# Reordered chunk work in the mLSTM heads, and its transfers issued by SyncE

## The chip, the core and the metric

The kernel runs as one program on one core of a Trainium2 chip. The metric is the device time of that program in microseconds (us). Five engines take part: TensorE (PE in the rows; PEld is its weight load), VectorE (DVE), ScalarE (ACT), GpSimd (POOL) and SyncE (SP), which here only issues transfers. Each has its own queue of instructions, worked off in order; they meet at semaphores.

## The reference, cut to what matters

Two layers of a decoder run over 1024 prompt tokens with 16 meta tokens ahead of them, and over 8 sample sequences of 4 tokens. The second layer is an mLSTM with 4 heads of width 512. The prompt goes in chunks of 128 tokens, one after another, because each chunk reads the matrix state C (512 x 512) that the chunk ahead left:

```python
num = w_inter[..., None] * jnp.einsum('bhtd,bhde->bhte', q, C) + jnp.einsum('bhts,bhse->bhte', s, v)
C_new = decay[..., None, None] * C + jnp.einsum('bhsd,bhse->bhde', k * w_s[..., None], v)
n_new = decay[..., None] * n + jnp.einsum('bhs,bhsd->bhd', w_s, k)
```

The first term of `num` is the **inter** part (through the old state), the second the **intra** part (within the chunk). Each of the 8 sample sequences has its own C of 1 MB a head, which is read, multiplied, updated and written back.

## The kernel before, in words

The stages run one after another: the attention layer, its output, the input projections of the mLSTM layer (`pre`), the four **heads** (function `heads`, from L1509), and the output stage (`post`). The change touches `heads` alone. For a head `e` it does this:

- **Values.** Nine tiles of 128 tokens (the first, of 48, holds sample and meta tokens): TensorE multiplies in three passes (high times high, high times low, low times high, helper `three`, L1690 to L1692) into banks 6 and 7 in turn; ScalarE copies the high part out (`high_v`, L1869), VectorE the low part (`low_v`, L1987). ScalarE and VectorE split the input x in the same way ahead of that (`high_x`, `low_x`), and the input c, which the projections need, at the last four tiles (`high_c`, `low_c`, tiles 5 to 8).
- **Projections.** Four blocks of keys and four of queries (`project`).
- **Chunks 0 to 7.** A chunk c has on TensorE: `scores`, `turn_keys` (transposes), `sample_parts` (reads the state `Cs` of sample c), then `inter` (four multiplications with C, with the four `sample_state` multiplications between them), `intra`, and `prompt_state` (four units of three passes). The results of `sample_state` and `prompt_state` are called units; they go alternately to banks 2 and 3, so that TensorE may write unit u only when VectorE has taken unit u-2 (`kv_done`). VectorE takes them in the order of its own code: `sample_states`, `numerator`, `prompt_states`. `numerator` is three instructions: inter part times a column (L2126), plus the intra part (L2127), and `bn_stats` on the sum (L2129).
- Chunk 0 has no inter part. Its `prompt_state` also adds the 48 first tokens (twelve more passes), and `small` makes some sums of one column and the sample sequences' own scores.
- After chunks 4 and 6 VectorE also splits the next head's weights (`low_w`, L1995).

**Transfers.** SyncE issues the loads of a head: c, the gate rows (`ub`, `nrow`, `ws`), `w_q`, and the next head's x, `w_k`, `w_v`. GpSimd issues all that belongs to the states: the loads of the sample states into the two halves of `Cs`, their stores, the stores of the numerators (`num`), and at a head's end C, n and the sample numerators. The load of c for head e+1 (L1621) waits for TensorE's last unit of head e; the gate rows wait for the stores of n.

Of the kernel before, what the change touches and what calls it, by code (L numbers as in the profile page):

```python
# [13 lines left out]
P = 128  # L14
# [1111 lines left out]
def seq(i):  # L1126

    return slice(SQ + P * i, SQ + P * (i + 1))
# [380 lines left out]
def heads(nc, d, const, cols, metaw, decay8, gate_dram, x_dram, ca_dram, num_dram, mv, den):  # L1509
# [5 lines left out]
    with ExitStack() as ctx:  # L1515
# [45 lines left out]
        kv_full, kv_done, small_full, small_done, num_full, num_done = (  # L1561
            s.sem(n) for n in ("kv_full", "kv_done", "small_full", "small_done", "num_full", "num_done"))
# [22 lines left out]
        def _(sp):  # L1585
# [44 lines left out]

            load_v(0)
            load_x(0)
            load_k(0)
            for e in range(HC):
                load_c(e)
                load_rows(e)
                load_w(e)
                load_q(e)
                if e + 1 < HC:
                    load_x(e + 1)  # L1640
                    load_k(e + 1)
                    load_v(e + 1)

        @block.gpsimd
        def _(pool):
            old = d["state_C"].rearrange("l b h (k p) c -> (l b) h p k c", p=P)
            new = d["out_C_s"].rearrange("l b h (k p) c -> (l b) h p k c", p=P)
            pool.memset(qm[:, :, :, :], 0.0).then_inc(qm_zero, 1)
            for e in range(HC):
                cc = slice(DH * e, DH * (e + 1))  # L1650

                def load(b):
                    pool.dma_start(Cs[:, b % 2], old[b, e]).then_inc(cs_in[b % 2], 16)

                def store_num(c):
                    pool.wait_ge(num_done, NT * e + c + 1)
                    pool.dma_start(num_dram[c, :, cc], num[:, c % 2, :]).then_inc(num_out[c % 2], 16)

                pool.wait_ge(p_full, NJ * (e + 1))
                for b in range(2):  # L1660
                    load(b)
                for b in range(B):
                    pool.wait_ge(kv_done, NU * e + s_unit(b, KH - 1) + 1)
                    pool.dma_start(new[b, e], Cs[:, b % 2]).then_inc(cs_out[b % 2], 16)
                    if b >= 1:
                        store_num(b - 1)
                    if b + 2 < B:
                        pool.wait_ge(cs_out[b % 2], 16 * (B // 2) * e + 16 * (b // 2) + 16)
                        load(b + 2)
                store_num(NT - 1)  # L1670
                pool.wait_ge(kv_done, NU * (e + 1))
                pool.dma_start(d["out_C_p"].rearrange("l b h (k p) c -> (l b h) p k c", p=P)[e], C[:, :, :]).then_inc(c_out, 16)
                with nc.allow_non_contiguous_dma(reason="512 words"):
                    for m in range(KH):
                        pool.dma_start(d["out_n_p"].rearrange("l b h (k p o) -> (l b h) p k o", p=P, o=1)[e, :, m],
                                       nall[:, m, NT - 1:NT]).then_inc(n_out, 16)
                pool.dma_start(d["out_n_s"].rearrange("l b h c -> (l b) (h c)")[:, cc], nrow[:, :]).then_inc(n_out, 16)
                pool.wait_ge(fold_done, e + 1)
                pool.dma_start(num_dram[NT, 0:NS, cc], s_num[:, :]).then_inc(snum_out, 16)
            for j in range(2):  # L1680
                pool.wait_ge(num_out[j], 16 * (NT // 2) * HC)
                pool.wait_ge(cs_out[j], 16 * (B // 2) * HC)
            pool.wait_ge(c_out, 16 * HC)
            pool.wait_ge(n_out, 16 * (KH + 1) * HC)
# [800 lines left out]
```

## Time and profile before

| | us |
|---|---|
| median of 3 runs | 2527.56 (2524.15 to 2535.24) |
| the profiled execution, whole | 2520.63 |
| its span in the trace | 2518.9 |
| TensorE busy in the span | 2147.9 (85%) |
| VectorE / ScalarE / GpSimd busy | 1096.5 / 632.9 / 94.4 |
| the heads, from the first value tile | 1446 to 2256 |

### The profile page before, as it was taken

How to read it: one execution, taken by the hardware profiler on the slowest of the kernel's cores; microseconds unless marked ns; L12 is line 12 of the kernel's file. 1: busy time of each engine (PE TensorE's matmuls, PEld its weight loads, DVE VectorE, ACT ScalarE, POOL GpSimd, SP SyncE). 2: the span in 40 equal slices, each digit the busy share in tenths (PEclk: the TensorE clock that was granted, in tenths of full speed). 3: DMA queues.
4: the chain of work that ended last, by engine and by line, in shares of the span. 5: the costliest groups of instructions: out<-in, count | busy, mean ns of one | idle time of the engine just before them, and what ended most of it. 6: DMA issues, size and time to landing. Idle time of an engine off the chain costs nothing. (4 is left out here: it accounts for less than half of the span.)

```text
span 2518.9 us, 28050 instructions
## 1 busy us (share of the span) xinstructions
PE 2147.9 (85%) x10945; PEld 1567.4 (62%) x10945; DVE 1096.5 (44%) x1868; ACT 632.9 (25%) x1088; POOL 94.4 (4%) x149
## 2 busy tenths in 40 slices
PE   4989888879956599899999598889889989965998
PEld 3655555544433244899999586576567558544885
DVE  4151515241222122353443345845764675566442
ACT  3151524240021111332222232121132122015221
POOL 0000000000000000000000000100110110110000
PEclk8999999989987799899999898998998899897999
DMA  3101010033066321586575413542542351448561
GB/s 114 28 24 39 11 51 0 18 95 113 0 183 207 122 67 39 91 114 155 128 132 148 192 71 108 185 148 101 177 180 91 130 184 37 144 156 296 180 184 34
DMA packets 180240, 281.80 MB, mean 112 GB/s; under 512 B 15283, under 2 KB 114615, under 8 KB 179018
## 3 DMA queue, kind: packets, MB, share of 16 engines
q1 hardware_dynamic: 151013, 183.12, 26.8%
q0 software_dynamic: 24256, 88.82, 9.8%
q10 hardware_dynamic: 4864, 8.39, 1.1%
q8 instruction: 72, 1.18, 0.2%
q14 instruction: 35, 0.29, 0.0%
HBM read 185.17 MB, written 95.31 MB: 111 GB/s over the span
## 5 line engine op out<-in xcount | busy, mean ns | idle before, releaser
L1263 PE MATMUL pre_ps<-x_xh,pre_wh 128*128 128x358 f32 (+1 forms) x792 | 260.0, 328 | 13.1 <-DVE pre_wl L1385 13.1
L1264 PE MATMUL pre_ps<-norm_xl,pre_wh 128*128 128x358 f32 (+1 forms) x792 | 258.5, 326 | 0.0
L1265 PE MATMUL pre_ps<-x_xh,pre_wl 128*128 128x358 f32 (+1 forms) x792 | 258.3, 326 | 0.0
L389 PE MATMUL attn_ps<-x_xnT,attn_w 128*128 128x512 f32 (+1 forms) x576 | 193.9, 498 | 9.9 <-DMA attn_w<-in_w_in_a 8.0
L389 PEld LDWEIGHTS attn_ps<-x_xnT,attn_w 128*128 128x128 f32 x576 | 97.1, 194 | 106.6 <-issue 98.4
L1263 PEld LDWEIGHTS pre_ps<-x_xh,pre_wh 128*128 128x128 f32 x792 | 149.5, 189 | 14.6 <-DVE pre_wl L1385 13.7
L1264 PEld LDWEIGHTS pre_ps<-norm_xl,pre_wh 128*128 128x128 f32 x792 | 149.5, 189 | 0.0
L1265 PEld LDWEIGHTS pre_ps<-x_xh,pre_wl 128*128 128x128 f32 x792 | 149.4, 189 | 0.0
L649 PE MATMUL pool_ps<-x_xnT,pool_w 128*128 128x512 f32 (+1 forms) x384 | 131.2, 505 | 13.8 <-DMA pool_w<-in_w_in_a 8.8
L1028 PE MATMUL norm_yp<-norm_wo,even_mixT 128*128 128x512 f32 (+1 forms) x288 | 127.8, 603 | 15.5 <-DMA norm_wo<-in_w_out_a 15.5
L1690 PE MATMUL head_ps<-head_ch,head_wh 128*128 128x358 f32 (+1 forms) x384 | 128.1, 334 | 12.2 <-issue 9.1
L2287 PE MATMUL post_ps<-post_woh,post_oh 128*128 128x512 f32 (+1 forms) x288 | 114.9, 399 | 17.1 <-DVE post_ol L2381 16.3
L1691 PE MATMUL head_ps<-head_cl,head_wh 128*128 128x358 f32 (+1 forms) x384 | 127.6, 332 | 0.0
L1692 PE MATMUL head_ps<-head_ch,head_wl 128*128 128x358 f32 (+1 forms) x384 | 127.2, 331 | 0.0
L2099 DVE SCALAR_TENSOR_TENSOR head_Cs<-head_Cs,head_ub,head_ps 128x512 f32<-128x512 f32 x128 | 93.9, 747 | 56.9 <-PE head_ps L1784 56.9
L1825 PE MATMUL head_ps<-head_C,head_q 128*128 128x512 f32 x224 | 117.2, 605 | 0.0
L649 PEld LDWEIGHTS pool_ps<-x_xnT,pool_w 128*128 128x128 f32 x384 | 65.5, 197 | 79.3 <-issue 70.4
L2288 PE MATMUL post_ps<-post_wol,post_oh 128*128 128x512 f32 (+1 forms) x288 | 113.3, 393 | 0.0
L2289 PE MATMUL post_ps<-post_woh,post_ol 128*128 128x512 f32 (+1 forms) x288 | 113.3, 393 | 0.0
L573 DVE TENSOR_TENSOR_SCAN attn_rest<-attn_neg 128x1040 f32<-128x1040 f32 (+8 forms) x72 | 89.9, 1249 | 47.1 <-ACT attn_neg L505 46.5
L1028 PEld LDWEIGHTS norm_yp<-norm_wo,even_mixT 128*128 128x128 f32 (+1 forms) x288 | 53.5, 188 | 84.2 <-issue 68.5
L1926 ACT ACTIVATE head_sTh<-head_sT 128x128 fp32r<-128x128 f32 x32 | 9.8, 308 | 364.6 <-DVE head_sT L2077 364.6
(374 smaller groups left out, 3803.7 us busy)
## 6 DMA issues: line engine op xcount, KB each, us to landing
head_Cs<-in_state_C POOLq DMA_DIRECT2D x32, 1024.0 KB, 5.8
out_C_s<-head_Cs POOLq DMA_DIRECT2D x32, 1024.0 KB, 4.7
x_xnT<-in_cache_sb_k SPq DMA_DIRECT2D x64, 256.0 KB, 2.9
pre_w<-in_w_in_c SPq DMA_DIRECT2D x32, 512.0 KB, 9.7
x_dram<-low_low SPq DMA_DIRECT2D x16, 536.0 KB, 9.7
ca_dram<-low_low SPq DMA_DIRECT2D x16, 536.0 KB, 10.6
b_dram<-pre_bv SPq DMA_DIRECT2D x16, 536.0 KB, 7.6
a_dram<-low_low SPq DMA_DIRECT2D x16, 536.0 KB, 7.6
```

Source lines behind the costliest of these rows:

```text
L389: last = pe.matmul(ps[:, bank + c, 0:c1 - c0], w[:, u, k, :], xnT[:, k, c0:c1], start=(k == 0), stop=(k == KD - 1))
L649: last = pe.matmul(ps[:, bank + c, 0:c1 - c0], w[:, g % 2, a, k, :], xnT[:, k, c0:c1], start=(k == 0), stop=(k == KD - 1))
L1028: last = pe.matmul(yp[0:rows, q, half, :], tok(mixT[:, k, :], i), wo[:, k, BANK * half:BANK * (half + 1)], start=(k == 0), stop=(k == KD - 1))
L1263: pe.matmul(out, wh[:, t % 2, k, :], xh[:, k, c0:c1], start=(k == 0), stop=False)
L1264: pe.matmul(out, wh[:, t % 2, k, :], xl[:, k, c0:c1], start=False, stop=False)
L1265: last = pe.matmul(out, wl[:, t % 2, k, :], xh[:, k, c0:c1], start=False, stop=(k == KD - 1))
L1690: pe.matmul(out, ah, bh, start=start, stop=False)
L1691: pe.matmul(out, ah, bl, start=False, stop=False)
L1692: return pe.matmul(out, al, bh, start=False, stop=stop)
L1825: pe.matmul(ps[:, 4, :], q[:, k, seq(c)], C[:, k, :], start=(k == 0), stop=(k == KH - 1))
L2287: pe.matmul(out, high, woh[:, k, c], start=(k == 0), stop=False)
L2288: pe.matmul(out, high, wol[:, k, c], start=False, stop=False)
```

## The change

1. **Chunk 0.** `prompt_state`, `small` and `intra` now come before `sample_parts` and `sample_state` on TensorE, and VectorE takes them in that order (`s_unit` and `c_unit` number the units anew to suit).
2. **Numerator.** ScalarE now does the multiplication of the inter part (`decayed`, a new function, between `high_keys(c)` and `own_keys(c+1)`); VectorE only adds. `bn_stats` (`moments`) comes after `prompt_states`.
3. **Split of c.** One tile earlier: tiles 4 to 7, and ahead of the copy of the tile's values instead of behind it.
4. **Head's end.** `low_x(e+1, 0)` and `low_x(e+1, 1)` come before the numerator of chunk 7. Value tile 0 uses bank 7, tile 1 bank 6, so that the wait for the denominators moves from tile 0 to tile 1.
5. **Transfers.** SyncE issues all that GpSimd did, in one queue with its loads. The state loads and stores of head e come after `load_v(e+1)`; the load of c for head e+1 comes after C's and n's stores of head e.

```diff
         def s_unit(b, m):
-            return 2 * KH * b + m
+            return 2 * KH * b + m + KH * (b == 0)
         def c_unit(c, m):
-            return 2 * KH * c + KH + m
+            return 2 * KH * c + m + KH * (c >= 1)
...
+            def states(e):
+                sp.wait_ge(p_full, NJ * (e + 1))
+                for b in range(2):
+                    load_state(e, b)
+                for b in range(B):
+                    sp.wait_ge(kv_done, NU * e + s_unit(b, KH - 1) + 1)
+                    sp.dma_start(new[b, e], Cs[:, b % 2]).then_inc(cs_out[b % 2], 16)
+                    if b >= 1:
+                        store_num(e, b - 1)
+                    if b + 2 < B:
+                        sp.wait_ge(cs_out[b % 2], 16 * (B // 2) * e + 16 * (b // 2) + 16)
+                        load_state(e, b + 2)
+                store_num(e, NT - 1)
+                sp.wait_ge(kv_done, NU * (e + 1))
+                sp.dma_start(d["out_C_p"].rearrange("l b h (k p) c -> (l b h) p k c", p=P)[e], C[:, :, :]).then_inc(c_out, 16)
...
                 load_w(e)
+                if e >= 1:
+                    store_sample(e - 1)
                 load_q(e)
                 if e + 1 < HC:
                     load_x(e + 1)
                     load_k(e + 1)
                     load_v(e + 1)
+                states(e)
...
                 if n == 0:
                     pe.wait_ge(wlv, e + 1)
                     if e >= 1:
-                        pe.wait_ge(den_done, e)
                         pe.wait_ge(parts_done, e)
+                elif n == 1 and e >= 1:
+                    pe.wait_ge(den_done, e)
...
+            def decayed(e, c):
+                act.wait_ge(i_full, (NT - 1) * e + c)
+                if c >= 2:
+                    act.wait_ge(num_out[c % 2], 16 * (NT // 2) * e + 16 * (c // 2))
+                    act.wait_ge(bn_done, NT * e + c - 1)
+                act.activation(num[:, c % 2, :], ps[:, 4, :], ACT.Copy, scale=hcol(Q_INTER, c, e)).then_inc(i_done, 1)
...
                 for n in range(NV):
                     if n + 2 < NV:
                         high_x(e, n + 2)
+                    if n >= KH and n < 2 * KH:
+                        high_c(e, n - KH)
                     high_v(e, n)
-                    if n >= NV - KH:
-                        high_c(e, n - NV + KH)
...
                 low_scores(e, 0)
                 log_weights(e, 1)
+                prompt_states(e, 0)
+                sample_small(e)
+                numerator(e, 0)
                 sample_states(e, 0)
-                sample_small(e)
-                prompt_states(e, 0)
-                numerator(e, 0)
+                moments(e, 0)
...
                     sample_states(e, c)
+                    if c == NT - 1 and e + 1 < HC:
+                        low_x(e + 1, 0)
+                        low_x(e + 1, 1)
                     numerator(e, c)
                     prompt_states(e, c)
+                    moments(e, c)
```

VectorE, one chunk from 1 on, before (`Cs` is a sample state, `C` the prompt's, `kwl` the keys' low part):

```order
L2091 SCALAR_TENSOR_TENSOR head_kwl<-head_ps,all_cols,head_kwh 128x512
L2099 SCALAR_TENSOR_TENSOR head_Cs<-head_Cs,head_ub,head_ps 128x512 x4
L2126 TENSOR_SCALAR head_num<-head_ps,all_cols 128x512
L2127 TENSOR_TENSOR head_num<-head_num,head_ps 128x512
L2129 BN_STATS head_bn<-head_num 128x6
L2109 SCALAR_TENSOR_TENSOR head_C<-head_C,head_ub,head_ps 128x512 x4
```

And now:

```order
L2112 SCALAR_TENSOR_TENSOR head_kwl<-head_ps,all_cols,head_kwh 128x512
L2120 SCALAR_TENSOR_TENSOR head_Cs<-head_Cs,head_ub,head_ps 128x512 x4
L2146 TENSOR_TENSOR head_num<-head_num,head_ps 128x512
L2130 SCALAR_TENSOR_TENSOR head_C<-head_C,head_ub,head_ps 128x512 x4
L2150 BN_STATS head_bn<-head_num 128x6
```

Of the three instructions between the sample's units and the prompt's, one is left there.

TensorE behind the scores of chunk 0, before (`qm` are the samples' queries, `kb` their keys, `ks` and `qn` belong to `small`):

```order
L1762 MATMUL head_ps<-head_q,head_kz 128x128 x4
L1772 MATMUL head_ps<-head_Cs,head_qm 32x512 x4
L1784 MATMUL head_ps<-head_vs,head_kb 128x512 x4
L1799 MATMUL head_ps<-head_ks,all_const 8x512
L1802 MATMUL head_ps<-all_const,head_qn 128x1 x7
```

And now, behind the same scores (the first five rows), then from the end of `small` to the end of the chunk:

```order
L1769 MATMUL head_ps<-head_q,head_kz 128x128 x4
L1696 MATMUL head_ps<-head_vh,head_kwh 128x512
L1697 MATMUL head_ps<-head_vl,head_kwh 128x512
L1698 MATMUL head_ps<-head_vh,head_kwl 128x512
L1696 MATMUL head_ps<-head_vh,head_kmh 128x512
```

```order
L1698 MATMUL head_ps<-head_vh,head_sTl 32x512
L1696 MATMUL head_ps<-head_vh,head_sTh 128x512
L1697 MATMUL head_ps<-head_vl,head_sTh 128x512
L1698 MATMUL head_ps<-head_vh,head_sTl 128x512
L1826 MATMUL head_ps<-all_const,head_sT 128x1
L1696 MATMUL head_ps<-head_vh,head_sTh 128x512
L1697 MATMUL head_ps<-head_vl,head_sTh 128x512
L1698 MATMUL head_ps<-head_vh,head_sTl 128x512
L1828 MATMUL head_ps<-all_const,head_sT 128x1
L1779 MATMUL head_ps<-head_Cs,head_qm 32x512 x4
L1790 MATMUL head_ps<-head_vs,head_kb 128x512 x4
```

The reading of `Cs` has moved from the first place to the last, and `intra` (the rows with `sTh`, 128x512) now follows `small` at once.

SyncE at the end of head 0, before:

```order
L1597 DMA head_w<-in_w_v 128x4x512
L1621 DMA head_cr<-ca_dram 128x4x1072
L1612 DMA head_ub<-gate_dram 128x1088
L1613 DMA head_nrow<-in_state_n 8x512
L1629 DMA head_ws<-gate_dram 128x1072
```

And now:

```order
L1647 DMA out_C_s<-head_Cs 128x4x512
L1639 DMA num_dram<-head_num 128x512 x2
L1655 DMA out_C_p<-head_C 128x4x512
L1658 DMA out_n_p<-head_nall 128x1 x4
L1660 DMA out_n_s<-head_nrow 8x512
L1621 DMA head_cr<-ca_dram 128x4x1072
L1612 DMA head_ub<-gate_dram 128x1088
```

The load of c (`cr`) now stands behind six issues that were another engine's.

## Rows read from the trace of the kernel before

**Rows 1.** Busy time of one stretch, the heads: PE, PEld, DVE, ACT, POOL, clock, DMA share, GB/s.

```profile
1446.00:2256.00 810.00, 726.07 (x3408) 530.72 (x3408) 500.47 (x829) 176.86 (x320) 80.86 (x123) 0.93 0.38 134
```

**Rows 2.** TensorE's waits in the heads (total us, times, longest), then one group by line.

```profile
PE head_ps L1690 <- DVE head_C L2109: 40.8, 28, 1.5
PE head_ps L1690 <- DVE head_xl L1981: 32.7, 4, 27.2
PE head_ps L1772 <- DMA head_Cs<-in_state_C: 16.6, 4, 4.8
...
L1690 PE MATMUL head_ps<-head_ch,head_wh 128*128 128x358 f32 (+1 forms) x384 | 128.1, 334 | 12.2 <-issue 9.1 <-DVE head_cl L1991 3.1
```

**Rows 3.** Timeline of VectorE, chunk 4 of head 0: start, length, instruction, [idle before].

```profile
1603.01 0.75 DVE L2126 TENSOR_SCALAR head_num<-head_ps,all_cols 128x512 f32<-128x512 f32 x1
...
1604.51 0.69 DVE L2129 BATCH_NORM_STATS2 head_bn<-head_num 128x6 f32<-128x512 f32 x1
1605.12 1.39 DVE L2109 SCALAR_TENSOR_TENSOR head_C<-head_C,head_ub,head_ps 128x512 f32<-128x512 f32 x2
```

**Rows 4.** Timeline of TensorE, from chunk 3's like release to chunk 4's.

```profile
1593.64 0.50 PE L1690 MATMUL head_ps<-head_vh,head_kwh 128*128 128x512 f32 x1 [1.47 <-DVE head_C L2109]
...
1600.91 1.02 PE L1825 MATMUL head_ps<-head_C,head_q 128*128 128x512 f32 x2
...
1604.06 0.39 PE L1692 MATMUL head_ps<-head_vh,head_kwl 128*128 128x512 f32 x1
1605.91 0.50 PE L1690 MATMUL head_ps<-head_vh,head_kwh 128*128 128x512 f32 x1 [1.47 <-DVE head_C L2109]
```

**Rows 5.** Chunk 0 of heads 0 to 3, scores to scores: us, PE busy, clock, DMA.

```profile
1525.92:1556.44 30.52, 25.18 (x100) 0.73 0.49 172
1727.21:1759.06 31.85, 27.09 (x99) 0.66 0.44 165
1930.51:1965.51 35.00, 29.84 (x99) 0.57 0.42 150
2136.50:2163.70 27.20, 23.69 (x100) 0.76 0.44 155
```

**Rows 6.** The same view of a stretch within head 3's chunk 0.

```profile
2151.00:2167.00 16.00, 16.00 (x45) 0.50 0.20 66
```

**Rows 7.** Timelines of TensorE and VectorE around `small`, head 0.

```profile
1538.75 1.72 PE L1802 MATMUL head_ps<-all_const,head_qn 128*128 128x1 f32 x14
1541.80 0.73 DVE L2115 SCALAR_TENSOR_TENSOR head_nrow<-head_nrow,all_decay,head_ps 8x512 f32<-8x512 f32 x1 [3.15 <-PE head_ps L1692]
1542.47 0.67 DVE L2116 COPY head_s_num<-head_ps 32x512 f32<-32x512 f32 x1
```

**Rows 8.** The first projections of heads 1 and 3: us, PE busy, clock, DMA.

```profile
1676.00:1713.00 37.00, 36.71 (x215) 0.95 0.30 108
2085.00:2122.00 37.00, 36.43 (x214) 0.95 0.06 24
```

**Rows 9.** Timeline of VectorE after chunk 4 of head 0.

```profile
1608.25 2.28 DVE L1995 TENSOR_TENSOR head_wl<-head_w,head_wh 128x2048 fp32r<-128x2048 f32 x1
```

**Rows 10.** The page's DMA issues (KB each, us to landing), then timelines of SP and ACT.

```profile
head_Cs<-in_state_C POOLq DMA_DIRECT2D x32, 1024.0 KB, 5.8
out_C_s<-head_Cs POOLq DMA_DIRECT2D x32, 1024.0 KB, 4.7
head_cr<-ca_dram SPq DMA_DIRECT2D x4, 2144.0 KB, 16.6
...
1645.55 0.37 SPq L1621 DMA_DIRECT2D head_cr<-ca_dram  x1
...
1665.46 1.09 ACT L1876 ACTIVATE head_ch<-head_cr 128x1072 fp32r<-128x1072 f32 x1
```

**Rows 11.** Timelines of POOL and SP around the end of the heads.

```profile
2256.22 0.53 POOL L1679 DMA_DIRECT2D num_dram<-head_s_num  x1
2269.45 0.32 SPq L2235 DMA_DIRECT2D post_num<-num_dram  x1
```

More of the change, by code:

```diff
@@ L1629, in load_w, with load_state, store_num, store_sample @@
                 sp.dma_start(ws[:, :], gate_dram[e:e + 1, XT + NT + B:GW].to_broadcast([P, XT])).then_inc(ws_in, 16)
+            old = d["state_C"].rearrange("l b h (k p) c -> (l b) h p k c", p=P)
+            new = d["out_C_s"].rearrange("l b h (k p) c -> (l b) h p k c", p=P)
+            def load_state(e, b):
+                sp.dma_start(Cs[:, b % 2], old[b, e]).then_inc(cs_in[b % 2], 16)
+            def store_num(e, c):
+                sp.wait_ge(num_done, NT * e + c + 1)
+                sp.dma_start(num_dram[c, :, DH * e:DH * (e + 1)], num[:, c % 2, :]).then_inc(num_out[c % 2], 16)
+            def states(e):
[13 more added lines that the diff above has]
+                sp.dma_start(d["out_C_p"].rearrange("l b h (k p) c -> (l b h) p k c", p=P)[e], C[:, :, :]).then_inc(c_out, 16)
+                with nc.allow_non_contiguous_dma(reason="512 words"):
+                    for m in range(KH):
+                        sp.dma_start(d["out_n_p"].rearrange("l b h (k p o) -> (l b h) p k o", p=P, o=1)[e, :, m],
+                                     nall[:, m, NT - 1:NT]).then_inc(n_out, 16)
+                sp.dma_start(d["out_n_s"].rearrange("l b h c -> (l b) (h c)")[:, DH * e:DH * (e + 1)], nrow[:, :]).then_inc(n_out, 16)
+            def store_sample(e):
+                sp.wait_ge(fold_done, e + 1)
+                sp.dma_start(num_dram[NT, 0:NS, DH * e:DH * (e + 1)], s_num[:, :]).then_inc(snum_out, 16)
             load_v(0)
@@ L1642, in _ @@
                     load_v(e + 1)
+                states(e)
+            store_sample(HC - 1)
+            for j in range(2):
+                sp.wait_ge(num_out[j], 16 * (NT // 2) * HC)
+                sp.wait_ge(cs_out[j], 16 * (B // 2) * HC)
+            sp.wait_ge(c_out, 16 * HC)
+            sp.wait_ge(n_out, 16 * (KH + 1) * HC)
+            sp.wait_ge(snum_out, 16 * HC)
         @block.gpsimd
         def _(pool):
-            old = d["state_C"].rearrange("l b h (k p) c -> (l b) h p k c", p=P)
@@ L1647, in _ @@
-            new = d["out_C_s"].rearrange("l b h (k p) c -> (l b) h p k c", p=P)
             pool.memset(qm[:, :, :, :], 0.0).then_inc(qm_zero, 1)
[L1649 to L1684, printed above, removed]
-            pool.wait_ge(snum_out, 16 * HC)
         @block.tensor
@@ L1705, in value_tile @@
                 for k in range(KH):
-                    last = three(ps[0:rows, 6 + n % 2, :], xh[:, k, c], xl[:, k, c], wh[:, 0, k, :], wl[:, 0, k, :], k == 0, k == KH - 1)
+                    last = three(ps[0:rows, 7 - n % 2, :], xh[:, k, c], xl[:, k, c], wh[:, 0, k, :], wl[:, 0, k, :], k == 0, k == KH - 1)
                 last.then_inc(v_full, 1)
@@ L1822, in inter @@
                 pe.wait_ge(num_done, NT * e + c)
+                if c >= 2:
+                    pe.wait_ge(i_done, (NT - 1) * e + c - 1)
                 for k in range(KH):
                     pe.wait_ge(kv_done, NU * e + c_unit(c - 1, k) + 1)
-                    pe.matmul(ps[:, 4, :], q[:, k, seq(c)], C[:, k, :], start=(k == 0), stop=(k == KH - 1))
+                    last = pe.matmul(ps[:, 4, :], q[:, k, seq(c)], C[:, k, :], start=(k == 0), stop=(k == KH - 1))
+                    if k == KH - 1:
+                        last.then_inc(i_full, 1)
                     sample_state(e, c, k)
@@ L1838, in _ @@
                 scores(e, 0)
+                prompt_state(e, 0)
+                small(e)
+                intra(e, 0)
                 sample_parts(e, 0)
@@ L1841, in _ @@
                     sample_state(e, 0, m)
-                small(e)
-                prompt_state(e, 0)
-                intra(e, 0)
                 for c in range(1, NT):
@@ L1868, in high_v @@
                 act.wait_ge(v_full, NV * e + n + 1)
-                act.activation(vh[0:rows, i, :], ps[0:rows, 6 + n % 2, :], ACT.Copy).then_inc(vh_done, 1)
+                act.activation(vh[0:rows, i, :], ps[0:rows, 7 - n % 2, :], ACT.Copy).then_inc(vh_done, 1)
             def high_c(e, k):
@@ L1965, in _ @@
                     high_keys(e, c)
+                    decayed(e, c)
                     if e + 1 < HC:
@@ L2152, in _ @@
             for e in range(HC):
-                low_x(e, 0)
-                low_x(e, 1)
+                if e == 0:
+                    low_x(e, 0)
+                    low_x(e, 1)
                 for n in range(NV):
@@ L2157, in _ @@
                         low_x(e, n + 2)
+                    if n >= KH and n < 2 * KH:
+                        low_c(e, n - KH)
                     low_v(e, n)
```

24 lines of the change are left out of this document (12 added, 12 removed).

## The prediction

> **What bounds the kernel now.** I read the page first: TensorE is busy for 85% of the span. Then the stretch of the heads, the only one that the change touches [rows 1]: 810 us, of which TensorE is busy for 726, VectorE for 500, ScalarE for 177. So TensorE sets this stage, and it can become shorter in two ways: its idle time (84 us) goes, or its clock, 0.93 on the mean, rises. Third, the waits of TensorE say whose fault the idle time is [rows 2]: 40.8 us in 28 waits are for VectorE's update of C, 32.7 for the low part of x (27.2 of them once, before head 0, which the change leaves alone, so 5.5 in three), 16.6 in four for the first sample state, and 12.2 before the first projection. Each of the four has its own edit. All the edits lie inside the 810 us.
>
> **The numerator (edit 2).** In a chunk VectorE does L2126, L2127, L2129 and only then the first update of C [rows 3]. TensorE has meanwhile finished two units of the prompt's state, at 1604.06 + 0.39 = 1604.45, and may start the third only at 1605.91, when the first has been taken [rows 4]: 1.47 us of idle, in each of the 28 chunks from 1 to 7. Now only the addition stands there. It could start at 1603.01, where L2126 does, if ScalarE's product is ready. The last inter multiplication ends at 1600.91 + 1.02 = 1601.93 and ScalarE has nothing else to do; the nearest row for its copy of 512 columns is the 0.75 of L2126, so the product is there at about 1602.8. The update of C then starts one spacing later (1604.51 to 1605.12 is 0.61), at 1603.65, and TensorE may go on 0.79 later (1605.12 to 1605.91), at 1604.44. That is when its second unit ends, so the whole 1.47 goes and the period, from 1593.64 to 1605.91 [rows 4] or 12.27 us, becomes 10.8, TensorE's own work. VectorE, busy for 500 of 810 us and rid of 28 times 0.75, can follow. In 25 chunks this is 25 x 1.46 = **36.4**. Not in the last chunk of heads 0 to 2: there the two `low_x` stand ahead of the addition, and they wait for ScalarE's product, its copy of the parts and its high parts of x. VectorE gets to the addition some 1.9 us later than it would, so the stall is about 1.9 us, 0.5 more than now: 3 x 0.5 = **-1.5**. And the cover of `low_w` becomes thin: it lasts 2.28 us [rows 9], `bn_stats` (0.69) now also stands ahead of it, and the chunk is shorter by 1.46. I work out a stall of 1.3 us at the third sample unit where now there is 0.3: six chunks, **-6.0**. `bn_stats` itself costs nothing elsewhere: VectorE waits there for the next scores.
>
> **The end of a head (edit 4).** With the low parts of x ready and the denominators no longer asked for, value tile 0 follows the last prompt unit at once: **+5.5** [rows 2]. Tile 1 gets its denominators: they take 0.7 us behind VectorE's last update, and tile 0 takes 2.9.
>
> **The split of c (edit 3).** Its last low part now comes before the last tile's values, so the first projection starts at once: **+12.2** [rows 2]. In heads 1 to 3 the clock is below 1.00 just behind that wait, 0.95 in 37 us in two of them [rows 8] and a little lower in the third, about 2 us of lost work each: **+6.0**.
>
> **Chunk 0 (edit 1).** Its four stretches add up to 124.6 us [rows 5]. In head 0, 30.52 us at a mean clock of 0.73 are 16.5 us at half clock, so the 25.18 us busy are 17 us of work at full clock; head 3 gives 17 as well. To these 17 the new order adds a wait for the keys' low part (new: the scores end and nothing stands between; about one VectorE instruction of 0.75 and two releases, 1.1), one of 1.5 (new: `intra` needs VectorE's 0.73 + 0.67 [rows 7], which `prompt_state` covered before), and some 1.4 for the samples' units, which go at VectorE's pace: 21.0 us, or 84 for four. The wait for `Cs` is gone, since the state has 13 us more to arrive in. So the gain is 41 us if the clock stays up. It did not stay up: it is 0.57 to 0.76 in these stretches, and in head 3, where TensorE was busy all the time, it stood at 0.50 for 16 us on end [rows 6]. What lay ahead of that fall was the thin work of `small`, 14 matmuls of one column in 1.72 us [rows 7], after a wait of 2.8 us. The new order still has `small`, with a wait right behind it, and then the narrow sample work. I expect a fall there too, later and partly over waits: 10 to 13 us at half clock, some 5 us lost a head. That gives 41 - 21 = **+20**. The ends are +41 (no fall) and +7 (a full fall of 17 us on dense work in each head, 4 x 8.5 lost).
>
> The Trainium skill, page "TensorE: Matmul & The Clock Gate", section "Why this matters for your kernels", says that idle gaps between bursts, such as a wait for a DMA, put the engine back to its lower rate. Head 3's row speaks against this as the whole story: the clock was low while nothing waited. By the rule alone, chunk 0 would give the 41 us.
>
> **The transfers (edit 5).** Most of it is hidden. A state's store and the next load on the same half of `Cs` take 4.7 + 5.8 = 10.5 us [rows 10]; from the sample's update to the next need for that half there are about 15 us in the shorter chunks, and 12 for the first. SyncE has nothing else queued in the chunks. The place to look at is the load of c for the next head. Before it was issued at 1645.55, 0.5 us behind TensorE's last unit, and landed 16.6 us later in the median [rows 10], at about 1662; ScalarE took it at 1665.46 and did not wait. Now six issues stand ahead of it on SyncE (C, four of n, one more), about 0.4 us each, and C's megabyte ahead of it in the queue; and ScalarE comes to it sooner: now 18.6 us behind the start of the value tiles, then a tile of 2.8 us earlier and some 2.0 us more because it goes ahead of the tile's copy, so 13.8 us behind the start, which is the end of the last unit; TensorE feels a delay from 1.5 us on. The bytes in flight are the same as before. If small stores of n no longer hold it up it lands at 13 to 14 us and costs nothing; if it keeps its longest landing of 17.5 us on top of an issue 3.3 us late, TensorE waits 6 us a head. I take 0.7 a head, nearer to the lower end since bandwidth is left over (DMA share 0.38 [rows 1]): **-2**, ends 0 and -18. Last, GpSimd's final store was issued at 2256.22 and the next stage started at 2269.45 [rows 11]; SyncE issues faster than the 0.53 us of GpSimd: **+2**, ends 0 and +5.
>
> "DMA: Bandwidth & Descriptors" in the Trainium skill, section "Issuing engines are not separate DMA queues", says that who issues changes only the time of the issue. That fits a small term here, and no run so far shows it.
>
> **Sum.** 36.4 - 1.5 - 6.0 + 5.5 + 12.2 + 6.0 + 20 - 2 + 2 = 72.6 us. The profiled execution took 2520.6, so it would take 2448. The median of the runs lies 7 us above the profiled one; I expect the same of the new kernel: **2455 us**.
>
> **The rivals.**
> *The clock stays up in chunk 0.* For it: three of the four waits for `Cs` were over 4 us and go. Against it: head 3. It gives 21 us more: 2434.
> *The clock falls as long as before, and c comes late.* For it: `small` is now followed by more narrow work; c's load is behind a queue. Chunk 0 gives 7 instead of 20 and c costs 18 instead of 2: 29 us less, 2484.
> *The stall changes its place.* The addition waits for ScalarE's product (it has a release from TensorE, 0.7 us of work and a release to VectorE in it), and edit 2 brings nothing: the 36.4 go, 2491. Against it: 1.1 us lie between the end of inter and 1603.01.
> *Slower than before: state loads come late in the single queue.* Each of the 24 reloads has a chain of store, numerator store, wait and load in one queue. It costs nothing up to 15 us and then each us costs TensorE one. All gains are spent when each reload is late by 72.6 / 24 = 3 us, a chain of 18 us where the rows give 10.5. Against it: the DMA share of 0.38.
>
> **How the numbers follow.** My forecast 60%, the clock up 15%, clock and c 10%, the stall in a new place 8%, slower 4%, and 3% for something smaller near no change. The range takes in the first three and the edge of the fourth: 2430 to 2490. A measurement of this kernel tells some 0.5% (12.6 us) from no change. Faster by more than that: 93%; within it 3%; slower 4%.
>
> **What would show it.** Of the profile of the changed kernel: the waits for the update of C should be about 3 instead of 28, near 1.9 us each; a chunk's period 10.8 us; no wait for `Cs` before chunk 0's parts, but one of 1.1 and one of 1.5 us in each; no idle time before the first projection and its clock at 1.00; chunk 0 from scores to scores near 26 us. A wait of ScalarE for the load of c, with TensorE idle at value tile 6, would show the c term larger. The prediction is wrong if the clock in chunk 0 is up all the time (too high) or if a transfer shows among TensorE's longest waits (too low).

## The result, and the profile after

The changed kernel takes **2460.06 us** (median of 4 runs, 2455.93 to 2475.11) where the kernel before took 2525.99 (4 runs, 2524.15 to 2535.24). The ratio is 0.9743, with a 95% interval of 0.9695 to 0.9791. The forecast was 2455 with a range of 2430 to 2490. The profiled execution took 2455.93 us, its span 2454.2, so 64.7 us less than the span before.

First the heads, in the view of [rows 1], then their chunks 0 in that of [rows 5]: us, PE, PEld, DVE, ACT, POOL busy, clock, DMA share, GB/s.

```profile
1446.00:2192.00 746.00, 700.49 (x3407) 514.26 (x3405) 473.33 (x784) 195.07 (x348) 0.00 (x0) 0.95 0.42 143
1521.56:1546.44 24.88, 21.79 (x99) 12.72 (x100) 11.40 (x25) 2.69 (x7) 0.00 (x0) 0.79 0.35 126
1709.73:1734.83 25.10, 21.92 (x99) 12.96 (x100) 11.39 (x25) 2.69 (x7) 0.00 (x0) 0.80 0.34 125
1900.14:1925.19 25.05, 22.11 (x100) 12.93 (x101) 11.43 (x25) 2.69 (x7) 0.00 (x0) 0.78 0.36 125
2089.54:2113.76 24.22, 21.00 (x100) 12.56 (x100) 11.40 (x25) 2.69 (x7) 0.00 (x0) 0.86 0.24 87
```

TensorE's idle time fell from 84 to 46 us, and its clock rose from 0.93 to 0.95. What it still waits for, as in [rows 2] (total us, times, longest), and then, from the groups by line, the first pass of the projections:

```profile
PE head_ps L1696 <- DVE head_vl L2008: 17.6, 3, 6.6
PE head_ps L1696 <- DVE head_C L2130: 7.4, 21, 1.5
PE head_ps L1790 <- DVE head_Cs L2120: 6.2, 13, 0.6
PE head_ps L1696 <- DVE head_s_num L2137: 6.1, 4, 1.5
PE head_ps L1696 <- DVE head_kwl L2112: 4.0, 4, 1.0
```

```profile
L1696 PE MATMUL head_ps<-head_ch,head_wh 128*128 128x358 f32 (+1 forms) x384 | 125.1, 326 | 0.0
```

The waits for C went from 40.8 to 7.4 us, those for the sample state and before the projections are gone. At the top stands one that was not there: VectorE's low part of the values, three times, 5.2 to 6.6 us each. It is the load of c. This is the boundary from head 0 to head 1 on SyncE, ScalarE, VectorE and TensorE, in order of time:

```profile
1627.48 0.39 SPq L1655 DMA_DIRECT2D out_C_p<-head_C  x1
1627.91 3.31 SPq L1658 DMA_DIRECT2D out_n_p<-head_nall  x4
1631.26 0.34 SPq L1660 DMA_DIRECT2D out_n_s<-head_nrow  x1
1631.76 0.39 SPq L1621 DMA_DIRECT2D head_cr<-ca_dram  x1
1640.62 0.33 SPq L1612 DMA_DIRECT2D head_ub<-gate_dram  x1
...
1646.66 1.10 ACT L1889 ACTIVATE head_ch<-head_cr 128x1072 fp32r<-128x1072 f32 x1 [6.53 <-DMA head_cr<-ca_dram]
...
1649.72 0.79 PE L1696 MATMUL head_ps<-head_wh,head_xh 128*128 128x512 f32 x1 [5.19 <-DVE head_vl L2008]
```

ScalarE stands at the split of c from 1640.1 on, and the next copy of a value tile is queued behind it; VectorE's low part follows that copy, and TensorE follows VectorE. The DMA windows of the same boundary say what the load was doing:

```profile
1628.00:1631.00 3.00, 3.00 (x15) 2.11 (x14) 2.10 (x9) 1.11 (x2) 0.00 (x0) 1.00 0.88 330
1631.00:1640.00 9.00, 9.00 (x38) 6.38 (x37) 5.44 (x17) 3.22 (x6) 0.00 (x0) 1.00 0.85 46
1641.00:1649.00 8.00, 3.53 (x16) 2.54 (x14) 1.21 (x2) 2.34 (x4) 0.00 (x0) 0.92 0.92 370
```

The store of C moves at 330 GB/s; then for 9 us the DMA engines count as busy at a share of 0.85 and move 46 GB/s; then c comes at 370. In the 9 us stand some 600 packets of four bytes, the 512 words of n among them, which themselves take 5 us of engine time out of 122; nearly all the rest are 75 packets of c, at 1.5 us each where they take 0.17 later on. So the load of c has begun and hardly moves while n, issued ahead of it on the same queue, is being stored. The gate rows (`ub`) wait for n's stores, and are issued at 1640.62: that is when these are over.

**Where the 64.7 us are.** From one `scores` to the next, the periods of the two traces give: chunks 0 124.6 to 99.3 us (25.3); chunks 1 56.4 to 45.1 (11.2); chunks 2 to 6 246.5 to 222.6 (23.9); chunk 7 of head 3 1.3; the three boundaries, from chunk 7 to the next head's first scores, 286.0 to 291.2 (**-5.2**); the start of head 0 3.4; from TensorE's end to the next stage's first load 16.7 to 13.8 (2.9); other stages 1.9.

### The profile page after: what moved, and what is told of

Same layout as the page of the kernel before. It is cut to its first block and busy times, and to the rows that moved or that the text cites. A ratio compares the mean times of both kernels' runs of the same rounds, so it can differ in the third digit from the quotient of the medians.

```text
span 2454.2 us, 28078 instructions
## 1 busy us (share of the span) xinstructions
PE 2120.6 (86%) x10945; PEld 1549.6 (63%) x10945; DVE 1073.3 (44%) x1840; ACT 651.4 (27%) x1116; POOL 12.8 (1%) x25
## 5 line engine op out<-in xcount | busy, mean ns | idle before, releaser
L1263 PEld LDWEIGHTS pre_ps<-x_xh,pre_wh 128*128 128x128 f32 x792 | 149.6, 189 | 14.6 <-DVE pre_wl L1385 13.7
L1697 PE MATMUL head_ps<-head_cl,head_wh 128*128 128x358 f32 (+1 forms) x384 | 125.1, 326 | 0.0
L1696 PE MATMUL head_ps<-head_ch,head_wh 128*128 128x358 f32 (+1 forms) x384 | 125.1, 326 | 0.0
L1698 PE MATMUL head_ps<-head_ch,head_wl 128*128 128x358 f32 (+1 forms) x384 | 124.9, 325 | 0.0
L1790 PE MATMUL head_ps<-head_vs,head_kb 128*128 128x512 f32 x128 | 96.5, 761 | 6.2 <-DVE head_Cs L2120 6.2
## 6 DMA issues: line engine op xcount, KB each, us to landing
x_dram<-low_low SPq DMA_DIRECT2D x16, 536.0 KB, 10.1
```

Source lines behind the costliest of these rows:

```text
L1263: pe.matmul(out, wh[:, t % 2, k, :], xh[:, k, c0:c1], start=(k == 0), stop=False)
L1696: pe.matmul(out, ah, bh, start=start, stop=False)
L1697: pe.matmul(out, ah, bl, start=False, stop=False)
L1698: return pe.matmul(out, al, bh, start=False, stop=stop)
```

## The experiments

All times are medians of 4 runs (e4 of 10), each beside runs of the kernel before (2522 to 2524); edits are against the changed kernel where nothing else is said.

**e1_c_first and e2_n_behind_c** move the load of c, **e3_pool_issues** and **e4_only_sync** take the transfers' part alone. In e1 c goes ahead of C's store, in e2 between C and n (head 0's c is then loaded ahead of the loop over the heads):

```diff
                 store_num(e, NT - 1)
+                if e + 1 < HC:
+                    load_c(e + 1)
                 sp.wait_ge(kv_done, NU * (e + 1))
```

```diff
                 sp.dma_start(d["out_C_p"].rearrange("l b h (k p) c -> (l b h) p k c", p=P)[e], C[:, :, :]).then_inc(c_out, 16)
+                if e + 1 < HC:
+                    load_c(e + 1)
                 with nc.allow_non_contiguous_dma(reason="512 words"):
```

> The changed kernel, but SyncE issues the load of c for the next head ahead of the stores of C and n of the head that ends (right behind the last numerator's store). Theory A (the 17.6 us that TensorE waits at value tile 6 in three heads come from the place of the load of c in the single queue): the load is issued within 1 us of TensorE's last unit, lands some 8 us later, ScalarE no longer waits for it, the three waits of 5.2, 6.6 and 5.9 us go, and with them the half-clock stretch of 6.8 us behind each: 20 to 26 us less than the changed kernel, about 2436. Theory B (the two splits that now stand ahead of the value copies hold TensorE up by themselves): the waits stay above 3 us each and the time stays within 8 us of 2460.

> The changed kernel, but the load of c for the next head stands between the store of C and the five stores of n, so that C's megabyte is still ahead of it and the 512 writes of 4 bytes are behind. Theory A1 (it is the small writes of n that hold the queue: while they run it moves 60 GB/s for about 9 us): c lands 3 us later than with c in front, some 11 us behind TensorE's last unit, before ScalarE asks for it at 13.8, and all the time of the other run is won, 2436 to 2440. Theory A2 (bytes and issue time of what stands ahead): C's store takes 2.8 of the 6 us, so about half of the wait stays, 2 to 4 us a head, and the time is 2446 to 2450.

e1: 2443.29 us, ratio 0.9679 (0.9643 to 0.9714). e2: 2438.65, 0.9676 (0.9643 to 0.9709). By the medians 16.8 and 21.4 us came back; the changed kernel's interval (0.9695 to 0.9791) is wide and just touches both, but the traces agree: the three boundaries take 274.5 and 271.1 us where they took 291.2. Part of it is clock: the three waits of the changed kernel are each followed by 6.8 to 10.2 us at half clock, and e2 has one such stretch left, of 3.4 us. e1 fell short of what was expected of it (20 to 26 us, no wait left): waits of 4.0 and 1.2 us for the value tile remain, in e2 one of 3.2. ScalarE at the first boundary, in e1, then in e2:

```profile
1647.26 1.10 ACT L1891 ACTIVATE head_ch<-head_cr 128x1072 fp32r<-128x1072 f32 x1 [5.36 <-DMA out_C_p<-head_C]
```

```profile
1644.93 1.10 ACT L1891 ACTIVATE head_ch<-head_cr 128x1072 fp32r<-128x1072 f32 x1 [4.55 <-DMA head_cr<-ca_dram]
```

In e1 c was in after 9 us, but its high part goes where C lies, and C's store now came last, 17.9 us after its issue and with n's stores right behind it. The two transfers must both be over, and at this boundary neither order frees the split; at the third boundary both do.

In e3 GpSimd issues the state transfers again, as before the change; e4 is the kernel before with only these functions moved to SyncE, so its diff is the same with the signs turned:

```diff
-                states(e)
-            store_sample(HC - 1)
...
         def _(pool):
...
+                for b in range(2):
+                    load(b)
+                for b in range(B):
+                    pool.wait_ge(kv_done, NU * e + s_unit(b, KH - 1) + 1)
+                    pool.dma_start(new[b, e], Cs[:, b % 2]).then_inc(cs_out[b % 2], 16)
...
```

> The changed kernel with edit 5 undone: GpSimd issues the states, numerators and final states as before, and SyncE only the loads; edits 1 to 4 stay. If the load of c lands as it did before (14 to 17.5 us behind its issue, 0.5 us behind TensorE's last unit) while it is asked for at 13.8, TensorE waits 1 to 4 us in each of three heads instead of 6: 7 to 12 us less than the changed kernel, 2448 to 2453, that is, edit 5 costs time on balance. Rival: the transfers by GpSimd delay sample states in the shorter chunks, so that waits for Cs come back and the time is over 2465.

> The kernel before with edit 5 alone: SyncE issues all, nothing else is changed. The load of c is asked for 20.4 us behind TensorE's last unit there and would land at about 20, so TensorE waits 0 to 1 us a head; the end of the heads stage is 3 us shorter; the wait for the first sample state keeps its 4 us: 2519 to 2528, no change that can be told. If the late load of c or the waits for Cs grow, it is slower than before by up to 15 us.

e3: 2450.38 us, 0.9721 (0.9689 to 0.9752), with two waits for the value tile of 6.1 us together instead of three of 17.6. e4: 2518.34, 0.9985 (0.9968 to 1.0003), with the waits of [rows 2] nearly as they were. **So the move to one queue costs nothing in the kernel before and, by the medians, 9.7 us in the changed one.** The intervals of e3 and the changed kernel overlap, so the size is not certain; the direction is borne out by the traces, in which the three boundaries take 275.5 us in e3 and 291.2 in the changed kernel (286.0 before, 285.7 in e4). The shorter boundary needs c earlier, and the move brings it later: 5.1 us behind TensorE's last unit instead of some 0.5.

**e5_numerator_undone, e6_chunk0_undone, e7_split_late** each take one edit back: in e5 VectorE multiplies the inter part again, with `bn_stats` right behind the sum; in e6 chunk 0 stands in its old order on TensorE and VectorE; in e7 c is split at value tiles 5 to 8 again.

```diff
-            act.activation(num[:, c % 2, :], ps[:, 4, :], ACT.Copy, scale=hcol(Q_INTER, c, e)).then_inc(i_done, 1)
...
+                    link(dve.tensor_scalar(dst, ps[:, 4, :], hcol(Q_INTER, c, e), None, ALU.mult))
```

```diff
-                prompt_state(e, 0)
-                small(e)
-                intra(e, 0)
                 sample_parts(e, 0)
                 for m in range(KH):
                     sample_state(e, 0, m)
+                small(e)
+                prompt_state(e, 0)
+                intra(e, 0)
```

```diff
-                    if n >= KH and n < 2 * KH:
-                        high_c(e, n - KH)
                     high_v(e, n)
+                    if n >= NV - KH:
+                        high_c(e, n - NV + KH)
```

> The changed kernel with edit 2 undone: VectorE multiplies, adds and takes bn_stats ahead of the prompt's units, ScalarE's decayed is gone; the rest stays. Theory (a third of a chunk's update stood in TensorE's way): the waits for the update of C come back in all 28 chunks, the period goes from 10.98 to 12.27 us, and the time rises by 25 x 1.29 = 32 us to 38 us, to about 2495. Rival (VectorE's order was not what set the period; the other edits would have brought it): the time rises by less than 15 us.

> The changed kernel with edit 1 undone: chunk 0 reads and updates the sample state first, then small, the prompt's units and intra. Theory (the wait for the first state, 4 times 3 to 5 us, and the 17 us at half clock that lie on the dense units): the four chunks 0 take 120 to 126 us again instead of 99, chunk 1 begins at half clock, and the time rises by 25 to 32 us to about 2488. Rival (the clock falls anyway, only elsewhere, so that only the wait itself counts): the rise is 10 to 15 us, about 2473.

> The changed kernel with edit 3 undone: the high and low parts of c are made at value tiles 5 to 8, behind the tile's copies; the load of c keeps its late place. Theory: c is asked for some 4.8 us later and TensorE feels a delay later still, so the waits at the value tiles shrink from 17.6 us to under 4, while the wait before the first projection comes back, 3 us in each of four heads: the two cancel, 2452 to 2462. Rival (the split's earlier place is worth its 12 us whatever c does): over 2468.

e5: 2488.7 us, 0.9860 (0.9837 to 0.9883); the period is 12.27 us again and 28 waits for C add up to 43.1. The numerator is worth 28.6 us, a little under the 32 to 38 expected. e6: 2494.27, 0.9881 (0.9860 to 0.9902); the four waits for the sample state are back (16.4 us), and chunk 0 takes 35.2, 35.0, 35.1 and 27.1 us. The order of chunk 0 is worth 34.2, over the 25 to 32 expected. e7: 2454.62, 0.9724 (0.9699 to 0.9749). Of its waits, the one ahead of the projections in heads 1 to 3:

```profile
PE head_ps L1696 <- issue: 9.1, 3, 3.0
```

The late split brings back 12.2 us ahead of the projections (these 9.1 and 3.1 in one head) and their lower clock (332 ns a matmul for 326). It cuts the waits for the value tile from 17.6 to 2.0 us, with no half clock behind them (23.9 us in the changed kernel, 3.4 in each of these heads now behind the projections' wait), and its median is 5.4 us *lower* than that of the changed kernel. The intervals overlap, so that it is faster is not shown; but no run shows a gain from edit 3 as the change has it. That it pays with c early is likely, since e2 has no wait ahead of the projections and only one of 3.2 us at a value tile, but no run has the late split with c early.

**e8 to e10: what brings the clock down in chunk 0.** In the changed kernel it is at half for 6.8 to 13.7 us in each chunk 0, from behind `small` (14 matmuls of one column) and a wait of 1.5 us for `s_num`. e8 is e2 with `small` between the second and the third prompt unit, so that VectorE has time for `s_num`; e9 is e8 with the one-column sums taken out of `small`, one to each later chunk; e10 is e2 with only this. The first diff is that of e8 and e9, the second that of e9 and e10:

```diff
-                prompt_state(e, 0)
+                prompt_state(e, 0, (0, 1))
                 small(e)
+                prompt_state(e, 0, (2, 3))
```

```diff
-                for c in range(1, NT):
-                    pe.matmul(ps[:, 6, 80 + c:81 + c], qn[:, P * (c - 1):P * c], one, start=True, stop=True)
...
                     intra(e, c)
+                    one_column(e, c)
                     prompt_state(e, c)
```

> The kernel with the load of c ahead of n's stores, and besides small stands between the second and the third of chunk 0's prompt units, on TensorE and on VectorE. Theory: the wait of 1.5 us at intra goes in each head (VectorE copies small's results under two units), 6 us in all, and the clock's fall, if thin work followed by a wait brings it about, comes later or is shorter: 6 to 15 us less than the kernel without this, 2424 to 2433. Rival (the thin work alone brings the fall about): the half-clock stretches in chunk 0 keep their 7 to 14 us and now lie on the two dense units, so only 0 to 3 us are won, or up to 5 lost.

> This is e8_small_between with the one-column sums of the function small taken out of it and spread: each later chunk's sum stands behind that chunk's second prompt unit, and the four for the sample rows in chunk 1. Theory (TensorE's fall to half clock is brought on by thin work, the one-column sums above all, also where the engine has no gap): in e8 the clock was at half for 13.7, 13.7, 27.3 and 13.7 us from right behind small, and chunk 0 took 25.7, 25.65, 29.6 and 25.7 us. With the sums gone from there most of the fall goes: at most 7 us at half in each head, chunk 0 at 18.5 to 21 us (at full clock its work is what 99 to 107 us in four heads less about half of 10 to 27 us each leaves), and the time 15 to 28 us under e8's 2442, 2414 to 2427. Rival 1 (the other thin work of the chunk, products with 8, 32 and 48 rows or columns, brings the fall by itself): chunk 0 stays at 24 to 27 us and the time within 5 us of e8's. Rival 2 (the sums bring it wherever they stand): falls turn up in the later chunks, the period there rises above 10.98 us, and the time is at or over e8's.

> This is e2_n_behind_c with the same one-column sums spread over the later chunks, and with small where the changed kernel has it. Here the waits for VectorE's kwl (1.0 us) and s_num (1.5 us) stand in chunk 0, as in the changed kernel, but the sums don't. If the sums bring the fall: the stretches at half clock in chunk 0 (10.2, 3.4 or 6.8, 10.2, 13.7 us) go, chunk 0 falls from some 25 to 20 us in each head, and the time is 10 to 20 us under e2's 2438.7, 2419 to 2429. If the waits bring it: chunk 0 is as in e2 and the time within 4 us of 2438.7, while e9, which has no such wait, is faster. If either is enough together with the thin products of 8 to 48 columns: both e9 and e10 stay where they were.

e8: 2442.21 us, 0.9672 (0.9639 to 0.9704). The wait for `s_num` is gone and nothing was won, as its rival had it. TensorE's timeline in head 0, then windows of TensorE alone (us, PE busy, clock, DMA):

```profile
1528.81 1.72 PE L1813 MATMUL head_ps<-all_const,head_qn 128*128 128x1 f32 x14
1530.46 0.41 PE L1815 MATMUL head_ps<-all_const,head_qs 128*32 128x1 f32 x8
1530.80 0.25 PE L1817 MATMUL head_ps<-all_const,head_sT 32*32 32x1 f32 x2
1530.98 0.63 PE L1698 MATMUL head_ps<-head_vh,head_sTh 32*32 32x512 f32 x1
```

```profile
1528.81:1542.00 13.19, 13.19 (x50) 0.58 0.07 28
```

TensorE has no idle moment from 1528.81 to 1542, nor in the 4.5 us ahead of that, back to a wait of 1.0 us for `kwl` that ends at 1524.29; and still its clock drops to half where the one-column sums end (a pass takes 0.63 instead of 0.39), now over the dense units. e9: 2416.95, 0.9582 (0.9551 to 0.9612). Chunks 0 of heads 0 and 3, then all four heads:

```profile
1520.71:1538.42 17.71, 15.95 (x78) 1.00 0.49 178
...
2048.94:2066.64 17.70, 15.94 (x77) 1.00 0.31 118
...
1449.00:2148.00 699.00, 673.79 (x3398) 1.00 0.43 153
```

Not one drop is left in this execution of the heads, and chunk 0 takes 17.7 us, some 7 less than in the changed kernel. The period of the other chunks grew by 0.24 us, the price of the sums there. e10, which has the wait of 1.5 us but not the sums, lies between what was expected for either cause alone: 2433.3, 0.9643 (0.9617 to 0.9669):

```profile
1522.38:1544.60 22.22, 18.94 (x77) 0.85 0.38 142
...
1534.00:1535.00 1.00, 1.00 (x6) 1.00 0.00 0
1535.00:1536.00 1.00, 0.02 (x1) 0.92 0.00 0
1536.00:1537.00 1.00, 0.46 (x1) 0.50 0.00 0
```

Here the clock drops within the wait and stays down for 7 us in head 0 (10 in the changed kernel). **So a drop came in all four chunks 0 with the sums and no wait (e8), and in all four with the wait and no sums (e10); without both (e9) it came in none**, and in one of four in e12 below. These are counts from one profiled execution each. That e8 gained nothing and e9 25 us against it shows that removing one of two causes can look like removing none.

**e11_n_late and e12_all.** e11 is e2 with the four stores of n put off until just ahead of the next load of q; e12 is e9 with the same.

```diff
+            def store_n(e):
                 with nc.allow_non_contiguous_dma(reason="512 words"):
...
                     store_sample(e - 1)
+                    store_n(e - 1)
                 load_q(e)
```

> This is e2_n_behind_c (C_p stored, then the load of C, then n) with the four stores of n's prompt part, 128 writes of four bytes each, put off on SyncE's queue until just before the next head's load of q. In e2 the load of C, issued at 1628.29, landed 13.4 us later (median), with those stores on the same queue behind it, and 3.2 us of waits at the first value tile were left with 3.4 to 10 us at half clock after them. Theory (the four-byte writes share the queue's engines with C's load and slow it although they are issued behind it): C lands 9 to 11 us after its issue, no wait for head_vl at the value tile, the half clock behind it gone, the time 3 to 8 us under e2's 2438.7. Rival (C's load takes as long as it does for its own 1 MB beside the store of 1 MB ahead of it): it lands 13 us after its issue as in e2 and the time is within 2 us of e2's. Rival with a loss: the writes now fall beside the prefetch of the next rows, and a wait for q, v or k of over 1 us turns up in chunk 4 or 5: 2 to 6 us more than e2.

> This is e9_spread_between with the four stores of n's prompt part put off on SyncE's queue as in e11_n_late. In e9 TensorE ran at full clock through all four heads and one wait of 2.5 us for head_vl was left at a first value tile; in e11 the wait was gone. Theory (the two edits touch different waits, so their gains add, less what the clock no longer loses): the wait is gone, no stretch at half clock between 1449 and 2148 us, the time 2 to 3 us under e9's 2416.95, 2413 to 2416. Rival (e11's 6.8 us against e2 came mostly from the half clock that followed the wait, of which e9 has none, and the stores now meet the prefetch of the next rows): within 1.5 us of e9's, 2415.5 to 2418.5. Rival with a loss: a wait of over 1 us for q, k or v turns up in a middle chunk, 2420 or more.

e11: 2431.85 us, 0.9634 (0.9609 to 0.9660). The wait for the value tile and the half clock behind it are gone; the three boundaries take 266.3 us. The load of c at the first boundary, in e2 and then in e11 (KB, us from issue to landing):

```profile
head_cr<-ca_dram SPq DMA_DIRECT2D x1, 2144.0 KB, 16.6
```

```profile
head_cr<-ca_dram SPq DMA_DIRECT2D x1, 2144.0 KB, 11.3
```

At the two other boundaries it landed after 10.1 and 10.3 us in e2, 9.9 and 10.2 in e11; e9 and e12 repeat the pattern (15.9, 10.1, 10.3 against 11.3, 9.9, 10.4). So n's stores behind c delay it at the first boundary alone; why there stays open. (In e11 the gate rows also no longer wait for n and come sooner.) What such stores do by themselves shows in e2 by windows of TensorE (us, PE busy, clock, DMA), at the first and the second boundary:

```profile
1639.00:1645.00 6.00, 5.78 (x25) 1.00 0.00 0
1823.00:1829.00 6.00, 6.00 (x28) 1.00 0.03 3
```

Nearly all of n's words have started by then, next to nothing moves, and yet the gate rows get their signal only at 1645.6 and 1829.4, and c at the first boundary its own only at 1644.9. e12: 2416.61 us, 0.9576 (0.9550 to 0.9603), within e9's interval. Its last wait for a value tile is gone, and the boundary with it takes 88.7 us instead of 91.5, but in this execution the clock fell once, in head 1's chunk 0, and cost 7.6 us:

```profile
1697.07:1722.33 25.26, 23.50 (x78) 0.66 0.35 124
1702.00:1703.00 1.00, 1.00 (x4) 0.86 1.04 387
1703.00:1719.00 16.00, 16.00 (x38) 0.50 0.19 70
```

Chunk 0 of the other heads took 17.7 us. The code is that of e9 there, and what TensorE did before is the same: a thin stretch of scores and the wait of 1.0 us for `kwl`, over at 1700.6. The same place can thus bring the drop or not. e9's four runs fall in two pairs, 2411 and 2413 us at a mean clock of 0.945, 2421 and 2422 at 0.940; the profiled one is the fastest, so the drop-free heads are its better case. e12's lie at 2415 to 2417. Whether its second edit adds anything to e9's can't be told from these; both are some 43 us below the changed kernel and 106 below the one before.

## Why the prediction was right, and where it was not

The median is 5 us from the forecast, and that it is so near is partly luck: two terms are off by more, by 11 and by 23 us in opposite directions. The prediction's own sign that it is too low, a transfer among TensorE's longest waits, did show.

**The numerator, +36.4: 32.3.** The mechanism is as told; in 18 chunks 0.16 of the 1.47 us stayed, and the period is 10.98 instead of 10.8. VectorE in chunk 5 of head 0, in the place of [rows 3], and TensorE:

```profile
1598.38 0.75 DVE L2120 SCALAR_TENSOR_TENSOR head_Cs<-head_Cs,head_ub,head_ps 128x512 f32<-128x512 f32 x1 [0.34 <-PE head_ps L1790]
1599.20 0.69 DVE L2146 TENSOR_TENSOR head_num<-head_num,head_ps 128x512 f32<-128x512 f32 x1
1599.99 1.43 DVE L2130 SCALAR_TENSOR_TENSOR head_C<-head_C,head_ub,head_ps 128x512 f32<-128x512 f32 x2
...
1600.79 0.50 PE L1696 MATMUL head_ps<-head_vh,head_kwh 128*128 128x512 f32 x1 [0.16 <-DVE head_C L2130]
```

From the addition to the update of C it is 0.79 us, where I took a spacing of 0.61 from [rows 3]; those 0.18 are the 0.16. ScalarE's product was in time (the line of `decayed`, L1952, runs at 1598.16 to 1598.85). The rival in which the stall changes place did not come. 25 x (12.27 - 10.98) = 32.3, and e5 gives 28.6. (25 x 1.46 is 36.5, not 36.4.)

**Last chunk of heads 0 to 2, -1.5: none** (stall 1.49, as before: the two `low_x` held the addition up by 1.5 us and not 1.9). **The cover of `low_w`, -6.0: -3.4.** The stall behind it is 0.63 us and not 1.3; the chunk takes 11.88 us against 10.99 (0.89 more), before 12.60 against 12.27 (0.33 more), so 6 x 0.56.

**The end of a head, +5.5: came. The split of c, +12.2 and +6.0: came, with 7.8 for the clock** (the three passes took 128.1, 127.6 and 127.2 us, now 125.1, 125.1 and 124.9). Before the projections TensorE no longer waits.

**Chunk 0, +20: 31.4.** 124.6 to 99.3 us is 25.3, where I worked out 104. The waits of 1.0 and 1.5 us came as told, the clock fell for 10.2, 10.2, 13.7 and 6.8 us, about as told. What I left out is chunk 1. In the kernel before all four falls outlast chunk 0, whose ends stand in [rows 5], here two of them, by windows of TensorE:

```profile
1744.00:1762.00 18.00, 18.00 (x50) 0.53 0.17 59
...
2150.00:2168.00 18.00, 18.00 (x52) 0.53 0.20 67
```

So chunk 1 took 13.6 to 14.4 us against a period of 12.3. Of the 11.2 us won there 5.2 are the numerator's, 6.1 the clock's.

**The transfers, -2 with ends 0 and -18: some -25. This is the step that failed.** The waits took 17.6 us, and the half clock that begins in them (6.8, 10.2 and 6.8 us) took about 7 more; e11, which removes both, is 28.2 us under the changed kernel by the medians and 25.0 by the three boundaries of the traces. Three things were wrong in the working. I let c land 13 to 14 us behind the last unit, some 10 to 11 after its issue, taking n's small stores for harmless once they were issued ahead. It landed 14.9 to 16.3 us after its issue, 20 behind the last unit at the first boundary; with n's stores out of the way, in e11, it takes the 9.9 to 11.3 I had assumed. I put six issues at 0.4 us each; four of them take 3.31 us together, so c is issued 5.1 us behind the last unit and not 3. And my worst end held the longest landing but not the clock that falls behind a wait. The rule of the Trainium skill quoted beside this term ("DMA: Bandwidth & Descriptors", "Issuing engines are not separate DMA queues") is borne out by e4, where the move alone is worth 0.15% and not certain; it says nothing of what stands ahead in the queue, and that was the cost: e2 and e11 change little else and give 21.4 and 28.2 us.

**The tail, +2: 2.9.** With the other stages' 1.9 us, which no edit explains, the measured terms are 32.3 - 3.4 + 5.5 + 12.2 + 7.8 + 31.4 - 25 + 2.9 + 1.9 = 65.6, against 64.7 seen.

**The rivals.** "The clock stays up in chunk 0" is false for this kernel, and e9 shows what it would have taken. By the rule alone of the Trainium skill ("TensorE: Matmul & The Clock Gate", "Why this matters for your kernels": idle gaps bring the lower rate) chunk 0 would have given 41 us. Neither drop follows from it: in e10 it came in a wait of 1.5 us, shorter than the gaps that the page warns of, and in e8 behind 6.5 us in which the engine was never idle. "c comes late" is what happened in full, and "the clock falls as long as before" did not; the two halves of that rival should have been priced apart. The state loads in one queue were never late: no wait for `Cs` is left.

## What to carry to other kernels

When an edit shortens a stretch, list the transfers that land in it with the time they must be there, and look at what is queued ahead of each: here 2 KB in four-byte writes held a load up for longer than a megabyte did. Price a wait on TensorE with the half clock that may follow it, and look for that clock in the stretch behind as well as in the one that is edited. A clock that falls for two reasons need not rise when one is removed: take both away before you drop the theory, and count the drops in more than one execution.

## What was not expected of the hardware

- 512 writes of four bytes, 2 KB in all, were over only 7 to 9 us after they had started. A load of 2 MB behind them in the queue moved at 46 GB/s meanwhile, where it ran at 370 afterwards (changed kernel); with the load ahead of them, the DMA engines stood nearly still for 6 us (share 0.00 and 0.03 in e2) before their completion was told. Issued behind the load they delayed its landing from 11.3 to 16.6 us at one boundary and not at the two others (e11, e2).
- Half clock without an idle moment: in e8 it began behind 1.7 us of one-column matmuls, and lasted 13.7 to 27.3 us in the four heads, although dense passes of 512 columns followed at once.
- The same instructions brought a drop of 17 us in one execution (e12, head 1) and none in another (e9). What decides it stays open.
